# Two of three branch products finish their last two weight chunks output tile by output tile

## The reference

```python
def first_block(x, ...):
    for l in range(DEPTH):                       # DEPTH = 2
        h = _rmsnorm(x, norm_g[l])
        ...                                      # y_a, y_b, y_c: 256 x 512 each
        gates = jax.nn.sigmoid(gate_logits + b_gate[l]).reshape(bn, s, N_BRANCH, d)
        merged = (gates[:, :, 0] * (y_a @ w_branch[l, 0])
                  + gates[:, :, 1] * (y_b @ w_branch[l, 1])
                  + gates[:, :, 2] * (y_c @ w_branch[l, 2]))
        x = x + merged @ w_out[l]
    return x
```

## Time and profile before

| | us |
|---|---|
| runs shown | 1107.46, 1108.37, 1114.04 |
| median | 1108.37 |
| the profiled execution | 1110.5 |
| its span in the trace | 1108.8 |
| TensorE busy | 1036.7 (94%) |
| VectorE busy | 796.4 (72%) |
| ScalarE busy | 595.0 (54%) |

### The profile page before, as it was taken

The page is one execution under the profiler, slowest core; times in us unless marked ns, Lnnn a source line. Parts: engine busy times, 40 slices in busy tenths (PEclk is TensorE's granted clock), DMA queues, the critical chain, the costliest instruction groups (busy, mean ns, idle before and its releaser), DMA issues.

```text
span 1108.8 us, 22497 instructions
## 1 busy us (share of the span) xinstructions
PE 1036.7 (94%) x9301; PEld 954.4 (86%) x9301; DVE 796.4 (72%) x1233; ACT 595.0 (54%) x824; POOL 80.5 (7%) x176
## 2 busy tenths in 40 slices
PE   6999999999999999998988898888999999999996
PEld 6878999999877899998988898777889799998885
DVE  6869677787877876787799688765678648465445
ACT  5675585344765566543556655325336437666332
POOL 8500000010000000042050000000000000000000
PEclk9999999999999999999989999988999999999999
DMA  8645553474655443457456431100255335565552
GB/s 299 177 131 150 142 148 108 136 250 152 189 162 155 137 145 102 150 170 237 137 139 172 117 116 41 41 22 21 96 154 187 117 114 180 174 181 189 190 192 74
DMA packets 72214, 160.62 MB, mean 145 GB/s; under 512 B 6853, under 2 KB 13184, under 8 KB 72112
## 3 DMA queue, kind: packets, MB, share of 16 engines
q1 hardware_dynamic: 68960, 150.59, 44.6%
q0 software_dynamic: 2832, 8.06, 2.6%
q10 hardware_dynamic: 320, 0.53, 0.1%
HBM read 158.11 MB, written 1.05 MB: 144 GB/s over the span
## 4 chain that ended last, share of the span: by engine, by line
PE 68%; DVE 21%; ACT 5%; issue 4%; DMA 1%; DVEq 0%; ACTq 0%; SPq 0%
PE psum L458 18%; PE psum L460 17%; PE psum L459 17%; DVE ring_lo L1308 5%; PE psum L832 2%; ACT ring_hi L2260 2%; PE psum L980 1%; DVE arena L1685 1%; PE psum L821 1%; DVE arena L1649 1%; DVE arena L1647 1%; PE psum L716 1%; PE psum L685 1%; PE psum L663 1%; DMA ring<-in_w_branch 1%
## 5 line engine op out<-in xcount | busy, mean ns | idle before, releaser
L1308 DVE TENSOR_TENSOR ring_lo<-ring,ring_hi 128x1024 fp32r<-128x1024 f32 (+4 forms) x288 | 347.5, 1225 | 207.9 <-ACT ring_hi L2260 202.4
L2260 ACT ACTIVATE ring_hi<-ring 128x1024 fp32r<-128x1024 f32 (+4 forms) x288 | 296.6, 1046 | 288.9 <-PE psum L460 268.0
L458 PE MATMUL psum<-hT,ring_hi 128*128 128x256 f32 x904 | 259.4, 287 | 11.7 <-DVE ring_lo L1308 4.0
L460 PE MATMUL psum<-hT,ring_lo 128*128 128x256 f32 x904 | 256.1, 283 | 0.0
L459 PE MATMUL psum<-hT,ring_hi 128*128 128x256 f32 x904 | 255.9, 283 | 0.0
L458 PEld LDWEIGHTS psum<-hT,ring_hi 128*128 128x128 f32 x904 | 173.1, 191 | 15.2 <-issue 12.1
L458 PE MATMUL psum<-ring_hi,hT 128*128 128x512 f32 (+3 forms) x480 | 169.7, 353 | 15.3 <-DVE ring_lo L1308 8.0
L459 PEld LDWEIGHTS psum<-hT,ring_hi 128*128 128x128 f32 x904 | 173.1, 191 | 0.0
L460 PEld LDWEIGHTS psum<-hT,ring_lo 128*128 128x128 f32 x904 | 173.1, 191 | 0.0
L459 PE MATMUL psum<-ring_lo,hT 128*128 128x512 f32 (+3 forms) x480 | 164.4, 343 | 0.0
L460 PE MATMUL psum<-ring_hi,hT 128*128 128x512 f32 (+3 forms) x480 | 164.4, 342 | 0.0
(11 more groups left out here) (445 smaller groups left out, 1412.5 us busy)
## 6 DMA issues: line engine op xcount, KB each, us to landing
ring<-in_w_in SPq DMA_DIRECT2D x96, 512.0 KB, 3.6
ring<-in_w_ff SPq DMA_DIRECT2D x64, 512.0 KB, 3.6
ring<-in_w_branch SPq DMA_DIRECT2D x24, 512.0 KB, 3.9
ring<-in_w_out SPq DMA_DIRECT2D x24, 512.0 KB, 3.4
ring<-in_w_in SPq DMA_DIRECT2D x16, 520.0 KB, 3.6
ring<-in_w_xkv SPq DMA_DIRECT2D x16, 512.0 KB, 3.7
ring<-in_w_in SPq DMA_DIRECT2D x12, 384.0 KB, 3.3
ring<-in_w_in SPq DMA_DIRECT2D x8, 528.0 KB, 3.6
```

The source lines that it names most:

```text
L458: mm(b, lhs[0], rhs[0], start=start, stop=False, **how)
L460: return mm(b, lhs[1], rhs[0], start=False, stop=stop, **how)
L1308: V.tensor_tensor(chunk_view(ring_lo, RAW, c), chunk_view(ring, RAW, c), plain(chunk_view(ring_hi, RING_HI, c)), ALU.subtract).then_inc(ev ...
L2260: AC(chunk_view(ring_hi, RING_HI, c), chunk_view(ring, RAW, c), ACT.Copy).then_inc(ev("whi_ready"), 1)
```

## The change

The last argument of the branches' call is dropped, so that `pair` has its default of 2 for i = 0, 1 and 2. For i = 2 that is the value it had.

```diff
                 def branch(i):
                     pe.wait_ge(ev("lo_made"), SPLITS1 * l + 2 * (i + 1))
-                    gemm_rows_T(("br", l, i), yT[:, 1 - i % 2, :, :, :], 4, lambda k: None, 1 + i // 2)
+                    gemm_rows_T(("br", l, i), yT[:, 1 - i % 2, :, :, :], 4, lambda k: None)
```

## The result

The change makes the kernel slower. The first runs gave a median of 1124.7 us against 1108.8 (ratio 1.013, 95% interval 1.009 to 1.017); run once more beside 29 runs of the kernel before, 1123.8 against 1110.7 (1.012, 1.009 to 1.014). The forecast was 1117.6 with a range to 1121.5: the sign is right, the size too small, and the time lies outside the range. The profiled execution took 1121.8 us, its span 1120.1, so 11.3 us more span than before. Single executions fall now and then into a slower state with a lower granted clock (one profiled execution, that of e7, took 1164.6 us at a mean clock of 0.84); they are left out of every comparison here.

What follows compares the result with a forecast made beforehand. The prediction took TensorE, busy 94% of the span, and what makes it wait as the bound. Its terms, 5.47 + 2.08 + 1.7 = 9.25 us, on a median of 1108.37 us gave 1117.6 us, range 1111.0 to 1121.5.

Steps and rivals of the forecast that it cites:

- Step 1: Ahead of B0's pair TensorE waits for chunk 59's low part, entering 2.60 us late in both layers.
- Step 2: Chunk 62, released only at B1's end, makes VectorE's low part of 66 start 5.47 and 2.08 us later.
- Step 3: At the output product no slack hides VectorE's delay, so all of it counts: 5.47 + 2.08 = 7.55 us.
- The DMAs: Chunks 64 and 68 are issued later; in layer 1 chunk 64 is 0.1 us late, taken as nothing.
- Step 4: Four longer pauses, before B0's pairs and output products, may lower TensorE's clock; one fall, 1.7 us, bounds none to 5.4.
- the third rival: The clock falls in two to four of the pauses: 7.55 + 5.4 = 12.95 us, so 1121.3 us; chance 0.24.
- Only the wait for 59: Only layer 0's wait ahead of B0's pair costs, 2.6 us, and layer 1 nothing: 1111.0 us; chance 0.08.
- Faster: B1's tiles fill up to 2.1 us earlier, removing the output products' pauses of 1.07 and 2.83 us: 1104.5 us; chance 0.03.

Runs made afterwards that it cites:

- e7: Kernel before the change, with VectorE's low parts from chunk 66 on in the order of e5; 1110.3 us against 1110.9, ratio 1.000.
- e3: Changed kernel, with chunk 59's high part and the low parts of 58 and 59 made ahead of gates(5); 1115.8 us, ratio 1.005.
- e10: Kernel before the change, with TensorE also waiting for the low part of 59 before it starts chunk 58 in B0; one run of 1116.6 us.
- e2: Changed kernel, with the new pair kept for B1 alone (1, 2, 2); 1116.4 us, ratio 1.005.
- e5: Changed kernel, high parts 59 to 61 and low parts 58 and 59 earlier, low parts from 66 on behind the banks; 1110.7 us, ratio 1.000.
- e1: Changed kernel, with the new pair kept for B0 alone (2, 1, 2); 1116.0 us, ratio 1.006.
- e11: As e1, with GpSimd's 24 relative bias DMAs held back till layer 1's output product is copied; 1123.0 us.
- e4: Changed kernel, with VectorE's low parts of 66 and 67 moved behind B1's first two banks; 1121.5 us, ratio 1.008.
- e9: e5 with chunk 70's high and low parts made earlier too; 1107.5 us, ratio 0.996 against the kernel before.
- e6: Changed kernel, with 22 matmuls into an unused bank between the waits for chunks 58 and 59 in B0; 1119.5 us, ratio 1.007.

## Why the prediction was right or wrong

**Step 1, the pair's wait for chunk 59:** right. 2.60 us later than before was the figure; the pause came out at 3.31 against 0.62, so 2.69, in both layers, and e3 and e10 show it by taking it away and by setting it alone.

**Step 2, the late release of 62 and VectorE's queue:** right, and its sizes with it. Less what the clock added in B0's pair (7.28 and 7.33 us against 5.83: 1.45 and 1.50), the stretches grew by 5.56 and 2.15 us, 7.71 in all; the terms were 5.47 and 2.08. e2 sets B1's part alone (2.9 us in layer 0).

**Step 3, nothing hides it:** right for the change. But the argument that VectorE's order sets only the output product's *start* was narrow: e5 moved that start by 1.3 and 1.0 us ahead of before and gained nothing, since the low part of 70 held TensorE up two chunks later.

**The DMAs, bounds 0 to 1 us:** right for the change as a whole, for a reason that wasn't given. The late transfers would cost layer 1 up to 2.4 us by themselves (e1 44.73 against e11 42.32); in the change the release of 62 is later still and hides them: chunk 66 of layer 1, issued at 514.47 us, landed 7.5 us later, at 522.0, and its high part started at 523.11, behind the release.

**Step 4, the clock, is the one that failed:** "I take one fall, 1.7", for four longer pauses. The signs said no more than that 2.83 us had left the clock alone and 3.12 had not, and all four pauses were forecast at 3.1 us or more. Two of them were measured on another scale, too: a row's pause counts from the end that the profile gives the last matmul, 0.28 us behind its start, while 262.3 - 259.2 = 3.1 counts from 0.12 us behind it. As a row shows it, that pause is 2.9 us by forecast and was 2.84, next to the one of 2.83 that had no fall behind it. So the output products' pauses were no longer than that one, and the clock fell behind three of four all the same. In the changed kernel and in the variants with the pause of 3.3 us (two profiles of the change, e1, e4, e10, e11) B0's pair took 7.1 to 8.5 us in place of 5.8, in both layers: the clock fell every time, which cost 1.3 to 2.7 us. Ahead of the output product, behind the 2.8 us, it fell in the change's first profile in both layers, in the second in layer 1 alone:

```profile
265.00:269.00 4.00, 3.68 (x20) 3.71 (x21) 3.79 (x7) 0.92 (x3) 0.00 (x0) 0.61 0.34 138
...
536.60:541.00 4.40, 4.39 (x20) 4.40 (x21) 4.13 (x7) 1.56 (x3) 0.00 (x0) 0.50 0.25 97
```

So there were four falls in the first profile, for 3.6 us (1.45, 1.50, 0.34 and 0.35), and three in the second, for 4.6 us (1.34, 1.47 and 1.76), where one of 1.7 was taken. The price was near 1.7 where no other pause took part of it back; the count was wrong. What is left of the 11.35 and 12.26 us counted to chunk 70 is 7.7 us in both profiles: the queue's part, 7.55 by forecast.

The rule on idle gaps that the prediction cites (none over about 3 us between bursts of matmuls: the Trainium skill's page "TensorE: Matmul & The Clock Gate", section "Why this matters for your kernels") spoke for the third rival. The trace agrees with it on the 3.3 us pauses, and goes past it on the pauses of 2.7 to 2.9 us ahead of the output product, of which 9 of 14 had a fall behind them. That rival's 1121.3 us came nearest of all, and its sum by stretches, 12.95 us, is close to the 11.4 to 12.3 measured.

The rest of the way to 1124 us is for the most part the sum's base. It was the median of three runs, 1108.4 us; 29 runs of the same kernel have 1110.7, so the profiled execution of 1110.5 was an ordinary one and the 2.1 us taken off were not due. From 1110.7 the recorded sum gives 1119.9 us and the counted cost 1122.0 to 1122.9, against 1123.8 measured beside these runs. What is left, about 1 us, is within the interval; the second block's clock, which differs from run to run, is the only other thing seen to move.

**The rivals.** Only the wait for 59 (1111.0): refuted by e2. Faster: refuted, and e9 shows that even without the costs there is no gain in it.

## What to carry to other kernels

A product that finishes its last chunks tile by tile must have all of them before its first matmul and keeps all of them to its last; where rings are short and queues are in order, look first at what stands behind those chunks on the engines that prepare them. When a change leaves TensorE a pause of 2.7 to 3.3 us in the midst of full work, count the fall of the clock as the likely case and not as a risk: here it came behind 21 of 26 such pauses. And when a wait is cured, follow the next two chunks before calling it a gain: here it took several moves in VectorE's queue and one in ScalarE's to make 0.4%. Whether chunk 70's move alone would have made it wasn't tried.

## What the runs showed of the hardware

- A pause of 3.3 us ahead of B0's pair, behind full work, let the granted clock fall in twelve cases of twelve (the change's two profiles, e1, e4, e10 and e11). Pauses of 2.7 to 2.9 us ahead of the output product did in 9 of 14, two of them in the same execution of e2 (2.83 us each), while two of 2.8 us in e3's had none. Matmuls into an unused bank held it at 1.00 through the pause in both layers (e6).
- A fall cost the matmuls behind it from 1.3 to 2.7 us, for the same pause in the same place (B0's pair in layer 0 took 7.28 us in one profile and 8.54 in another, and 5.83 at full clock).
- A transfer of 512 KB started by SyncE landed in 3.2 us with none of GpSimd's loads beside it and in 8.3 us beside them, as e11 and e1 show for chunk 66 of layer 1.
